# Output stage of a hybrid encoder layer: transposes moved from TensorE to strided loads and VectorE

## The reference

```
y = jax.nn.gelu(y.reshape(bsz, seqlen, S5_WIDTH))
return y * jax.nn.sigmoid(y @ w_glu.astype(f32) + b_glu.astype(f32))
...
mix = jnp.concatenate([y_ssd, y_s5], axis=-1).astype(dtype) @ w_out[i]
x = _layer_norm(DEEPNORM_ALPHA * x.astype(f32) + g1 * mix.astype(f32), ln1_g[i], ln1_b[i]).astype(dtype)
h = (x.astype(f32) * (1.0 + sc2) + sh2).astype(dtype)
f = _moe(h, w_router, b_router, w_gate[i], w_up[i], w_down[i])
```

## Time and profile before

| what | value |
|---|---|
| median of 3 runs | 3408.94 us (3406.17 to 3411.16) |
| the profiled execution | 3409.89 us, of which the span from first to last instruction 3407.9 |
| mean granted TensorE clock | 0.945 |
| busy, share of the span | TensorE 89%, VectorE 39%, GpSimd 33%, ScalarE 20% |
| `mix_out`, first load to last logits copy | 1340.58 to 1903.37 us of the span |

### The profile page before, as it was taken

One profiled execution on the slowest core, in us unless ns is written; L12 is line 12 of the kernel. 1 busy time (PEld: TensorE's weight loads), 2 busy tenths in 40 slices (PEclk: granted clock), 3 DMA queues, 4 the chain that ended last, 5 costly groups with the idle time before them and its releaser, 6 DMA issues. The chain is left out here.

```text
span 3407.9 us, 33525 instructions
## 1 busy us (share of the span) xinstructions
PE 3024.5 (89%) x10104; PEld 1593.3 (47%) x10105; DVE 1335.2 (39%) x1910; ACT 668.4 (20%) x1382; POOL 1108.0 (33%) x1135
## 2 busy tenths in 40 slices
PE   7999999996688685899999379999999999999990
PEld 3555564563366464455554244444444444444440
DVE  2855245233788794333333622222222222222226
ACT  1112222222488211011111001111111111111106
POOL 0034676664466100222222122222222222222216
PEclk8999999997899897999999589999999999999995
DMA  6202433336336696422221143454444454442218
GB/s 258 81 37 81 137 102 94 102 101 270 114 118 185 144 228 194 155 93 99 96 96 50 63 181 101 150 169 128 125 125 123 123 171 149 123 123 49 49 37 314
DMA packets 147622, 437.81 MB, mean 128 GB/s; under 512 B 18953, under 2 KB 64265, under 8 KB 138561
## 3 DMA queue, kind: packets, MB, share of 16 engines
q1 hardware_dynamic: 79202, 282.27, 24.2%
q0 software_dynamic: 21168, 66.08, 8.7%
q10 hardware_dynamic: 47152, 88.20, 7.6%
HBM read 297.44 MB, written 139.03 MB: 128 GB/s over the span
## 5 line engine op out<-in xcount | busy, mean ns | idle before, releaser
L2111 PE MATMUL bank<-wg,exp_ht 128*128 x1008 | 455.0, 594 | 15.0 <-DVE exp_ht L2194 15.0
L2129 PE MATMUL bank<-wd,exp_hid_t 128*128 x1008 | 442.9, 592 | 0.9 <-ACT exp_hid_t L2165 0.9
L2111 PE MATMUL bank<-wu,exp_ht 128*128 x1008 | 442.9, 592 | 0.0
L2215 DVE TENSOR_TENSOR exp_out<-bank,exp_gates 128x512 f32<-128x512 f32 x126 | 81.2, 686 | 778.2 <-PE bank L2129 778.2
L2070 POOL DMA_INDIRECT x<-exp_out,exp_rows x63 | 102.7, 1630 | 869.9 <-DVE exp_out L2215 825.9
L1653 PE MATMUL bank<-mix_wo,mix_yt 128*128 128x512 f32 x768 | 342.0, 599 | 19.2 <-issue 11.6
L573 PE MATMUL bank<-x_t,w_in 128*128 128x512 f32 x768 | 338.2, 599 | 5.4 <-DVE x_t L481 5.4
L573 PE MATMUL bank<-w_in,x_t 128*128 128x264 f32 (+1 forms) x1152 | 339.6, 455 | 0.0
L2129 PEld LDWEIGHTS bank<-wd,exp_hid_t 128*128 128x128 f32 x1008 | 191.4, 190 | 241.6 <-issue 241.6
L2111 PEld LDWEIGHTS bank<-wu,exp_ht 128*128 128x128 f32 x1008 | 191.5, 190 | 241.1 <-issue 241.1
L2111 PEld LDWEIGHTS bank<-wg,exp_ht 128*128 128x128 f32 x1008 | 188.0, 192 | 227.2 <-issue 227.2
(11 more groups left out here) (357 smaller groups left out, 3658.2 us busy)
## 6 DMA issues: line engine op xcount, KB each, us to landing
wg<-in_w_gate SPq DMA_DIRECT2D x16, 2048.0 KB, 7.5
wu<-in_w_up SPq DMA_DIRECT2D x16, 2048.0 KB, 8.9
wd<-in_w_down SPq DMA_DIRECT2D x16, 2048.0 KB, 8.1
x_t<-in_x_t SPq DMA_DIRECT2D x6, 2048.0 KB, 8.4
mix_xt<-in_x SPq DMA_DIRECT2D x6, 2048.0 KB
x<-mix_v ACTq DMA_DIRECT2D x24, 512.0 KB, 2.6
h<-mix_h ACTq DMA_DIRECT2D x24, 512.0 KB, 2.6
com_v<-x SPq DMA_DIRECT2D x24, 512.0 KB, 6.6
```

The lines of the kernel that those rows point to most:

```text
L2111: mul = pe.matmul(bank[:, :], ht[:, j, k, :], flat(of[:, bass.ds(e % 2, 1), k * DE:(k + 1) * DE]), start=k == 0, stop=k == KT - 1)
L2129: mul = pe.matmul(bank[:, :], hid_t[:, j, k, :], flat(wd[:, bass.ds(e % 2, 1), k * D + q * WIDE:k * D + (q + 1) * WIDE]), start=k == 0, st ...
L2215: dve.tensor_tensor(out[:, j, q * WIDE:(q + 1) * WIDE], bank[:, :], gates[:, j, q * WIDE:(q + 1) * WIDE], ALU.mult).then_inc(out_read, 1)
```

## The change

No transpose is left on TensorE. The channels are cut into four quarters. SP loads y so that quarter q of a token's channels lies on partitions 32 q to 32 q + 31: for each of 16 groups of 32 tokens one DMA of 128 pieces of 512 bytes. VectorE's transpose of 32 x 32 blocks then gives channels on partitions (`turn_y`, 8 a wide). h is stored as before, read back from memory in the same manner (4 DMAs a tile, 128 pieces of 1 KB) and turned by VectorE (`turn_h`, one a tile). The weights are laid out on the host in the same order of channels, and `norm_w` is multiplied into `wo` once. The logits take `wr` as the stationary side on four strips of 32 columns (`strips_of`), and a product with a selection matrix `pick` adds the four up (`logits_of`). The gate products of the next wide (`glu`) stand behind the third tile, ahead of the fourth tile's products. The weights are loaded from ScalarE's queue, and all loops are written out.

```
 def mix_out(nc, C, S, y_ssd, yg, x, mod, W, x1_dram, h_dram):
...
             @block.sync
...
-                sp.wait_ge(turned, EVENTS)
-                load_y(1)
-                load_x(1, 1)
-                with sp.Fori(1, TURNS) as t:
-                    for j in range(2):
-                        m = t * 2 + j
-                        sp.wait_ge(turned, m * EVENTS)
-                        sp.nop(nofuse=True)
-                        load_y(m)
-                        sp.wait_ge(ln, (m - 1) * TPW * LN)
-                        sp.nop(nofuse=True)
-                        load_x(m, j)
+                def load_y(to, of, m, here):
+                    by_quad = of[wide_rows(m), :].rearrange("(a t) (q c) -> a q t c", t=SUB, q=QUADS)
+                    for a in range(WIDE // SUB):
+                        sp.dma_start(to[:, a, :], by_quad[a]).then_inc(here, 16)
...
+                def load_h(n):
+                    sp.wait_ge(h_stored[n % 2], (n // 2 + 1) * 16)
+                    if n >= 2:
+                        sp.wait_ge(h_turned, n - 1)
+                    by_quad = h_dram[tile_rows(n), :].rearrange("(g t) (q c) -> g q t c", t=SUB, q=QUADS)
+                    for g in range(QUADS):
+                        sp.dma_start(hq[:, n % 2, g, :], by_quad[g]).then_inc(hq_here[n % 2], 16)
+
+                load_y(yb, yg, 0, yb_here)
+                load_y(ya, y_ssd, 0, ya_here)
+                load_x(0)
+                for m in range(NWIDE):
+                    if m + 1 < NWIDE:
+                        sp.wait_ge(y_turned, m * TILES_A_WIDE + KY)
+                        load_y(yb, yg, m + 1, yb_here)
+                        sp.wait_ge(y_turned, (m + 1) * TILES_A_WIDE)
+                        load_y(ya, y_ssd, m + 1, ya_here)
+                        if m:
+                            sp.wait_ge(ln, (m * TPW - 1) * LN + 2)
+                        load_x(m + 1)
+                    for a in range(TPW):
+                        load_h(m * TPW + a)
...
             @block.vector
...
+                def turn_y(m, k, of, at):
+                    if k == 0:
+                        dve.wait_ge(ya_here if at == 0 else yb_here, (m + 1) * 16 * WIDE // SUB)
+                        if m >= 2:
+                            dve.wait_ge(mixed, (m - 1) * TPW)
+                    dve.transpose(yt[:, m % 2, at + k, :].rearrange("p (a t) -> p a t", t=SUB),
+                                  of[:, :, k * SUB:(k + 1) * SUB]).then_inc(y_turned, 1)
+
+                def gate(m, k):
+                    dve.wait_ge(glu_mm, (m + 1) * KY)
+                    dve.wait_ge(sig_done, m * KY + k + 1)
+                    to = yt[:, m % 2, KY + k, :]
+                    dve.tensor_tensor(to, sg[:, k, :], to, ALU.mult).then_inc(gated, 1)
+
+                def turn_h(n):
+                    dve.wait_ge(hq_here[n % 2], (n // 2 + 1) * 16 * QUADS)
+                    if n >= 2:
+                        dve.wait_ge(strips_mm, n - 1)
+                    dve.transpose(ht[:, n % 2].rearrange("p k (g t) -> p g k t", g=QUADS),
+                                  hq[:, n % 2].rearrange("p g (k c) -> p g k c", c=SUB)).then_inc(h_turned, 1)
...
+                for of, at in ((yb, KY), (ya, 0)):
+                    for k in range(KY):
+                        turn_y(0, k, of, at)
+                dve.wait_ge(w_here, C.mix_loads)
+                for k in range(KY):
+                    dve.tensor_scalar(wo[:, k, :], wo[:, k, :], norm_w[:, k:k + 1], None, ALU.mult).then_inc(prepared, 1)
+                for t in (ln_g, ln_b):
+                    dve.tensor_scalar(t[:], t[:], ALPHA, None, ALU.mult).then_inc(prepared, 1)
+                for k in range(KY):
+                    gate(0, k)
+                dve.wait_ge(prepared, KY + 4)
+                for m in range(NWIDE):
+                    for a in range(TPW):
+                        normalise(m, a)
+                        if m + 1 < NWIDE:
+                            for k in range(a % 2 * 2, a % 2 * 2 + 2):
+                                turn_y(m + 1, k, *((yb, KY) if a < 2 else (ya, 0)))
+                        if m or a:
+                            turn_h(m * TPW + a - 1)
+                    if m + 1 < NWIDE:
+                        for k in range(KY):
+                            gate(m + 1, k)
+                turn_h(NT - 1)
...
             @block.tensor
...
+                def products(m, a):
+                    n = m * TPW + a
+                    if a == 0:
+                        pe.wait_ge(gated, (m + 1) * KY)
+                        pe.wait_ge(y_turned, (m + 1) * TILES_A_WIDE)
...
+                def strips_of(n):
+                    pe.wait_ge(h_turned, n + 1)
+                    if n:
+                        pe.wait_ge(strips_taken, n)
+                    for i in range(KT // QUADS):
+                        for s in range(QUADS):
+                            k = s * (KT // QUADS) + i
+                            mul = pe.matmul(strip_bank[strip(s), 0:P], wr[:, k, :], ht[:, n % 2, k, :], start=i == 0, stop=i == KT // QUADS - 1)
+                    mul.then_inc(strips_mm, 1)
...
+                for m in range(NWIDE):
+                    for a in range(TPW):
+                        n = m * TPW + a
+                        products(m, a)
+                        if n >= 3:
+                            logits_of(n - 3)
+                        if n >= 2:
+                            strips_of(n - 2)
+                        if a == 2 and m + 1 < NWIDE:
+                            glu(m + 1)
...
             @block.scalar
...
+                for n in range(NT):
+                    m, a = divmod(n, TPW)
+                    if n >= 3:
+                        keep(n - 3)
+                    if n >= 2:
+                        take_strips(n - 2)
+                    if a == 2 and m + 1 < NWIDE:
+                        sigmoid(m + 1)
+                    store(n)
...
```

More of the change, by code:

```diff
@@ L1504, in _ @@
             def _(sp):
[L1505 to L1514, removed]
@@ L1524, in _ @@
[L1524 to L1531, removed]
@@ L1612, in in_order @@
-            def in_order(turn_gate, products, turn_h, logits):
-                def wide(m, j, more=True, first=False):
-                    for a in range(TPW):
-                        products(m, j, a, 0)
-                        if a >= 2:
-                            logits(m, a - 2)
-                        elif not first:
-                            logits(m - 1, a + 2)
-                        products(m, j, a, 1)
-                        if a:
-                            turn_h(m, a - 1)
-                        elif not first:
-                            turn_h(m - 1, TPW - 1)
-                    if more:
-                        turn_gate(m + 1, 1 - j)
-                return wide
+                steps = Steps(dve, ln)
@@ L1641, in turn_gate @@
                     for c in range(KY):
[L1642 removed]
+                        if m * KY + c >= 2:
+                            pe.wait_ge(sig_done, m * KY + c - 1)
                         for k in range(KY):
[L1644 to L1656 removed]
@@ L1675, in _ @@
-                pe.wait_ge(gate_here, C.mix_gate_loads)
-                wide = in_order(turn_gate, products, turn_h, logits)
-                turn_gate(0, 0)
-                pe.wait_ge(w_here, C.mix_loads)
-                wide(0, 0, first=True)
-                wide(1, 1)
-                with pe.Fori(1, TURNS - 1) as t:
-                    for j in range(2):
-                        wide(t * 2 + j, j)
-                wide(NWIDE - 2, 0)
-                wide(NWIDE - 1, 1, more=False)
-                logits(NWIDE - 1, TPW - 2)
@@ L1729, in _ @@
-                act.wait_ge(gate_here, C.mix_gate_loads)
-                wide = in_order(turn_gate, products, turn_h, logits)
-                turn_gate(0, 0)
-                wide(0, 0, first=True)
-                wide(1, 1)
-                with act.Fori(1, TURNS - 1) as t:
-                    for j in range(2):
-                        wide(t * 2 + j, j)
-                wide(NWIDE - 2, 0)
-                wide(NWIDE - 1, 1, more=False)
-                logits(NWIDE - 1, TPW - 2)
-                turn_h(NWIDE - 1, TPW - 1)
@@ L1742, in _ @@
+                keep(NT - 3)
+                for n in range(NT - 2, NT):
+                    take_strips(n)
+                    keep(n)
                 for r in range(2):
```

259 lines of the change are left out of this document (115 added, 144 removed).

## The result

The changed kernel takes 3468.19 us (median of 4 runs, 3461.92 to 3474.79) against 3410.05 of the kernel before, measured beside it: ratio 1.0171, 95% interval 1.0156 to 1.0186. It is slower by 58 us.

A forecast was written before the change was run, and what follows sets the result against it. TensorE sets the pace. Start 18.4, middle 3.0, late h 38.4 and end 7.7 sum to 67.5 us on the profiled 3409.89, which is 0.95 above the median: 3477 us, range 3420 to 3530 (the forecast case's own 3455 to 3505).

The forecast's parts named there:

- The two mechanisms: In the changed stage: a gate wait made by VectorE's order, and y and h loads on four of 16 DMA engines.
- second rival: Spread loads: y and h use 16 engines, no h wait, start 49.6 us, time 3421 us; chance 0.11.
- Start: First load to first product: weights and y loads, turns, scaling and gates take 62.6 us against 44.2, +18.4.
- Strips and logits: TensorE's logits on four column strips plus the small product: 1.2 us a tile, bounds 0.54 to 1.85 for the strips.
- Gate wait: Before a wide's first product TensorE waits on VectorE's normalisation, turns and gates: 14.0 us, of which strips and logits fill 1.2.
- four gates, 2.50: Last step of the gate wait's chain: VectorE's four gate multiplications take 2.50 us.
- h late: In four wides the first tile's turned h comes late behind y loads: wait 7.2 and clock 2.4 us each, +38.4.
- Clock behind the gates: TensorE runs at granted clock 0.50 after each long wait, charged at 2.4 us.
- End: After the last product, h of the last tile goes through memory: 28.1 us against 20.4, +7.7.
- first rival: Dearer packets: each DMA packet costs 1.2 to 1.7 times as much, time 3516 to about 3615 us; chance 0.16.

The follow-up runs named there:

- e2: The change with VectorE's last ya turns and the four gates moved from behind the fourth to behind the third normalisation, loads unchanged: 3456.54 us.
- e3: The change with both edits, y and h loads cut by quarter and the gates moved behind the third normalisation: 3340.32 us, ratio 0.9790.
- e1: The change with y and h loads cut by quarter of the channels, so 32 rows are outermost in the source: 3421.28 us, ratio 1.0043.
- e10: e1 with GpSimd's second operation on h (the shift) of each wide's fourth tile waiting until the four gates are done: 3417.40 us.
- e5: The change with only the loads of h cut by quarter (32 rows outermost), y loads unchanged: 3435.72 us, ratio 1.0074.
- e7: e1 with GpSimd's two operations on h made one-input, leaving out h's scale and shift: 3420.30 us, ratio 1.0030.
- e8: e1 with 16 added TensorE products into an unread bank while it waits for the gates: 3415.32 us, ratio 1.0010.
- e6: e1 with 14 added TensorE products into an unread bank while it waits for the gates: 3421.85 us, ratio 1.0042.

## Why the prediction was right, and where its terms were off

- **The two mechanisms hold.** The gate wait comes from gates behind the fourth normalisation: e2 and e3 move them and it is gone. The four engines hold y and h: the completions and the DMA share of 0.29 show it, and e1 takes the cost away. The second rival's 3421 is e1's time (3421.28), and its start of 49.6 e1's 49.5; in its middle a longer gate wait and cheaper strips happen to cancel.
- **Start, 18.4 predicted, 16.7 measured (60.95 - 44.2).** ya was turned 52.1 us after the first load, against 53.2.
- **Strips and logits, 1.2 taken, 0.8 measured**, within the bounds. 16 records on four strips take 0.65, a little over the lower bound of 0.54.
- **Gate wait, 12.8 predicted (14.0 less 1.2), 14.8 measured.** The mis-sized step is "four gates, 2.50": that row stands where GpSimd is idle. Beside GpSimd's work they take 4.72; e10 moves that work away, and they take 2.58.
- **h late, 38.4 predicted, 22.4 measured.** This is the term that was furthest off. In the wide shown the strips started 1638.61 - 1573.02 = 65.6 us after the fourth tile's products, against 67.2 predicted, and TensorE was ready for them at 62.0 instead of 60.0, since the gates, the clock and the tiles had taken longer. Both errors are small; they add up in the wait, which is the difference of the two times and falls from 7.2 to 3.6. The four waits are 15.6 together, and the gate products behind them lose 6.9 of clock (15.36, 15.55, 15.38 and 16.60 against 14.00), not 2.4 each.
- **Clock behind the gates, 2.4 taken:** the first 32 records took 16.76, 16.94, 17.03, 16.95 and 15.86, so 1.9 to 3.0.
- **End, 7.7 predicted, 7.1 measured.**
- **What the first rival had (dearer packets) did not come on four engines:** y took 14.29 and 13.81 for 14.0. On 16 a packet was dearer: at the 184 GB/s of e1's window 1 MB takes 5.7 us, where the second rival had 3.5.

In sum the stage lost 54.5 instead of 67.5, and the time came out at 3468 for 3477 (the sum as written gives 3476.4). The mechanism was right; that the number came so near is in part luck, for the errors of the middle have both signs: h late -16.0, strips and logits -8.4 (0.4 on 21 tiles), gate wait +10.0, clock behind the gates +1.5, and some +2 because a tile's products took up to 13.84 for 13.74.

## What to carry to other kernels

Before a load is cut into many small ones, look at the outermost dimension of its access pattern as well as at the size of its pieces: with 4 outermost it used four engines here, with 32 all 16, and h's loads in e5 are as many and their pieces as large. Where two waits lie behind each other in a loop, undoing one may show almost nothing (8.6 us) though the pair is worth 125: test them together. A duration is taken from a row with the same neighbours on the other engines, and a wait that is the small difference of two long chains (62.0 and 65.6) has the error of both.

## What was not expected of the hardware

- VectorE's product of two tensors in SBUF took 2.82 us beside a GpSimd operation and 0.68 without. The Trainium skill ("SBUF — State Buffer", Who interferes with whom) says that only one port pair, shared by VectorE and GpSimd, makes engines wait for each other, and that it is locked and not divided. The trace agrees for GpSimd's two-input operation: the second gate ended 0.55 us behind it. With a one-input operation on GpSimd that lasted 3.12 us (e7) the third gate took 1.52 and the fourth, wholly inside that operation, 0.68, which is no full lock.
- Behind a TensorE wait of 0.9 us (e8) or 1.5 the granted clock was 1.00; behind 2.6 (e6) four wides of five lost 1.70 us, behind 3.6 to 4.5 (h in the change) 1.4 to 2.6, behind 14.8 from 1.7 to 3.0. In these runs what the clock costs hardly grows with the wait. Why one wide in e6 kept its clock stays open.
- The same pieces of 512 bytes moved at 20.8 GB/s an engine on four engines and at 11.5 on 16 (the windows of the change and of e1). What holds the 16 back no run here tells apart.
